# Attention of the first chunk: the masked product of the turned probabilities on VectorE from PSUM instead of on GpSimd

## The reference

```python
dist = BLOCK + qi - si
valid = (dist >= 0) & (dist < WINDOW) & ((blk - 1) * BLOCK + si >= 0)
...
s = s - slopes[:, :, None, None] * dist.astype(jnp.float32)
s = jnp.where(valid, s, NEG_INF)
p = jax.nn.softmax(jnp.concatenate([s, sink_col], axis=-1), axis=-1)[..., :-1]
return jnp.einsum('...kgqs,...skd->...qkgd', p, v.astype(jnp.float32))
```

## Time and profile before

| what | value |
| --- | --- |
| median of 3 runs | 1970.55 us (1965.48 to 1975.21) |
| the profiled execution's own time | 1968.85 us |
| its span, first to last instruction | 1967.1 us |
| PE busy over the span | 1907.0 us (97%) |
| DVE, ACT, POOL busy | 1093.1 (56%), 898.1 (46%), 684.0 us (35%) |
| mean granted TensorE clock | 0.991 |

### The profile page before, as it was taken

The page is one execution under the profiler, slowest core; times in us unless marked ns, Lnnn a source line. Parts: engine busy times, 40 slices in busy tenths (PEclk is TensorE's granted clock), DMA queues, the critical chain, the costliest instruction groups (busy, mean ns, idle before and its releaser), DMA issues.

```text
span 1967.1 us, 27562 instructions
## 1 busy us (share of the span) xinstructions
PE 1907.0 (97%) x10556; PEld 1712.4 (87%) x10556; DVE 1093.1 (56%) x1889; ACT 898.1 (46%) x1794; POOL 684.0 (35%) x605
## 2 busy tenths in 40 slices
PE   7989999999999999999999999999999999999997
PEld 4767887687889998899999879999997999999796
DVE  7974416755693417546833474694337459441834
ACT  6764435645573214445732353573225347431532
POOL 0135675876122123521221262222126222212531
PEclk9999999999999998999999999999999999999998
DMA  6667885377676773466767526776763676777255
GB/s 231 246 236 264 300 311 164 129 279 252 244 263 207 262 253 131 151 236 253 279 229 275 212 108 247 266 271 240 280 222 107 229 282 244 256 274 249 103 207 177
DMA packets 110482, 451.01 MB, mean 229 GB/s; under 512 B 14836, under 2 KB 55060, under 8 KB 66324
## 3 DMA queue, kind: packets, MB, share of 16 engines
q1 hardware_dynamic: 110352, 449.25, 63.8%
HBM read 362.69 MB, written 86.52 MB: 228 GB/s over the span
## 4 chain that ended last, share of the span: by engine, by line
PE 76%; DVE 11%; ACT 4%; DMA 3%; issue 3%; POOL 2%; SPq 0%; POOLq 0%; DVEq 0%; ACTq 0%
PE psum L1337 66%; PE psum L1425 3%; PE psum L1393 3%; PE psum L1408 2%; DVE conv_out L1027 2%; DMA w_stage<-w_big 1%; DMA w_split<-w_cache 1%; PE psum L1369 1%; DVE inv_rms L996 1%; DVE lru_or_o L1060 1%; POOL w_split L597 1%; DVE scores L1126 1%; DVE resid L1096 1%; DVE gate_i L1044 1%; PE psum L1349 1%
## 5 line engine op out<-in xcount | busy, mean ns | idle before, releaser
L1337 PE MATMUL psum<-b_hi,w_split 128*128 128x384 f32 (+2 forms) x2880 | 811.0, 355 | 7.8 <-POOL b_lo L627 3.8
L1337 PE MATMUL psum<-a_hi,w_split 128*128 128x384 f32 (+2 forms) x2560 | 722.1, 356 | 11.7 <-DVE a_lo L990 6.7
L1337 PEld LDWEIGHTS psum<-b_hi,w_split 128*128 128x128 f32 x2880 | 532.9, 189 | 60.9 <-issue 23.1
L1337 PEld LDWEIGHTS psum<-a_hi,w_split 128*128 128x128 f32 x2560 | 472.0, 188 | 45.5 <-issue 12.6
L1337 PE MATMUL psum<-b_lo,w_split 128*128 128x384 f32 (+2 forms) x1440 | 504.7, 350 | 0.0
L1337 PE MATMUL psum<-a_lo,w_split 128*128 128x384 f32 (+2 forms) x1280 | 447.4, 350 | 0.0
L606 POOL TENSOR_TENSOR square_sum<-square_sum,square 128x384 f32<-128x384 f32 (+2 forms) x140 | 155.4, 1110 | 427.1 <-ACT square L769 427.1
L1337 PEld LDWEIGHTS psum<-b_lo,w_split 128*128 128x128 f32 x1440 | 272.3, 189 | 11.8 <-issue 0.4
L1337 PEld LDWEIGHTS psum<-a_lo,w_split 128*128 128x128 f32 x1280 | 241.2, 188 | 17.9 <-issue 4.2
L616 POOL TENSOR_TENSOR gate_tanh<-gate_tanh,lru_or_o 128x384 f32<-128x384 f32 (+1 forms) x80 | 87.1, 1090 | 337.0 <-DVE gate_tanh L1079 330.7
L769 ACT ACTIVATE square<-resid 128x384 f32<-128x384 f32 (+2 forms) x140 | 77.4, 553 | 261.0 <-DVE resid L1252 173.6
(11 more groups left out here) (169 smaller groups left out, 2479.8 us busy)
## 6 DMA issues: line engine op xcount, KB each, us to landing
w_split<-w_cache SPq DMA_DIRECT2D x272, 1024.0 KB, 4.8
w_cache<-w_split SPq DMA_DIRECT2D x68, 1024.0 KB, 6.6
w_stage<-w_big SPq DMA_DIRECT2D x68, 512.0 KB, 5.6
w_split<-w_cache_small SPq DMA_DIRECT2D x64, 256.0 KB, 4.4
x_stage<-x SPq DMA_DIRECT2D x32, 192.0 KB, 5.5
resid<-x SPq DMA_DIRECT2D x4, 1536.0 KB, 9.8
y_out<-resid SPq DMA_DIRECT2D x3, 1536.0 KB, 10.3
w_cache_small<-w_split SPq DMA_DIRECT2D x16, 256.0 KB, 6.2
```

The source lines that it names most:

```text
L1337: ins = nc.tensor.matmul(bank(g, c), W[:, s, w, k, :], x[:, k, 0:tt], start=(k == 0 and n == 0), stop=(k == nk - 1 and n == 2))
```

## The change

In the first chunk `keep_old` leaves POOL's program. DVE's program gets a `keep_old` of its own, which reads the turned probabilities from the PSUM bank that ACT copies from, and not from ACT's copy. It waits for the same semaphore, ACT's copy of the unit, and counts up the same one, `pt_old`. It stands after the scores of u + 2 and ahead of the unit's gate work. The other four chunks are left as they were.

```diff
@@ block.gpsimd, attention(g) @@
-                    keep_old(g, u)
+                    if g:
+                        keep_old(g, u)
@@ block.vector @@
+            def keep_old(g, u):
+
+                dve.wait_ge(pt_ready.sem, pt_ready.at(g, event(g, u) + 1))
+                v.tensor_tensor(PT[:, 1, :].rearrange("p (i q) -> p i q", i=4),
+                                PSUM[:, 6 + u % 2, :].rearrange("p (i q) -> p i q", i=4),
+                                OLD_T[:].unsqueeze(1).to_broadcast([128, 4, BLK]), ALU.mult).then_inc(pt_old.sem, 1)
@@ block.vector, attention(g) @@
                     if u + 2 < nu:
                         unit_scores(g, u + 2)
+                    if g == 0:
+                        keep_old(g, u)
                     if u - 3 in whole:
                         silu(g, KT + whole[u - 3])
```

## The result

The changed kernel takes 1975.98 us (median of 13 runs, 1974.54 to 1979.41) against 1970.43 for the kernel before (13 runs, 1965.48 to 1975.21). The ratio is 1.0032, its 95% interval 1.0024 to 1.0040: within the half per cent that the prediction calls no change, but the interval excludes 1, so the change costs about 5.5 us. The profiled execution has a span of 1972.9 us (before 1967.1) and a mean granted clock of 0.989 (0.991). "Turn u" is the start of unit u's turn on PE.

The account below looks back on a forecast made before the run. PE was taken as the bound (76% of the chain, period 4.79 us). Terms 0.74 + 3.60 + 1.67 + 1.3 - 1.13 - 1.73 = +4.45 us gave 1973.3 to 1975.0, forecast 1974 us (chance 0.50), range 1964 to 1982.

Parts of the forecast that it names:

- divide of unit 1, held (turn 1): First chunk: unit 0's weight split runs first on POOL and DVE's next divide waits for it; next turn +1.67 us.
- units 3 and 8, two gate operations (turns 4, 9): DVE's queue with product and two gate operations: ready at 5.16 us against a period of 4.79; +0.74 us for both.
- units 5 and 10, held divide (turns 6, 11): POOL's split starts when silu ends and holds the next divide, 1.80 us late each; +3.60 us for two.
- unit 13, gate product ahead of the divide: POOL's second gate product starts within 0.05 us of DVE's divide; whichever is first, about +1.3 us.
- late POOL products, units 6 and 14: PE's waits ahead of these units' values for POOL's late product disappear: -1.13 and -1.73 us.
- The product's price: Each 128x512 product on DVE takes 0.69 us, like the residual add, 0.60 in the queue; none above 0.75.
- The overtaking splits: Without the product POOL's weight splits start before DVE's divides in units 0, 5 and 10: +1.67 and +3.60 us.
- Units 2 and 7: No gate work, so DVE's divide is due 0.18 us ahead of POOL's split: no cost, but narrowly.
- all splits win: Rival, chance 0.13: units 2 and 7 also lose their 0.18 us, 1.58 each; +7.6 us, 1976.5 to 1978.2.
- DVE becomes the bound: Rival, chance 0.12: the product costs 1.364 us on DVE, from POOL's exclusion or the broadcast; +12.9 us, 1981.7 to 1983.4.
- Only the gain: Rival, chance 0.25: divides go ahead of splits in units 0, 5, 10 and 13; -1.8 us, 1967.0 to 1968.7.
- I pass the shift on whole: After the stage: the output projection moves along with PE's last unit, so the stage's whole +4.45 us reaches the kernel's time.

Follow-up runs that it names:

- the new order of PE alone: Kernel before, product still on POOL, with PE doing the values of u - 1 ahead of the turn of u in the first chunk: 1971.96 us, ratio 1.0018.

## Why the prediction was right, and what it left out

The time came out 2 us above the forecast, by the forecast's mechanism: the medians differ by 5.55 us, the sum had 4.45. Each term, as the distances between turns show it in the profile after against the profile before, in us:

| term | predicted | measured |
| --- | --- | --- |
| divide of unit 1, held (turn 1) | +1.67 | +1.76 |
| units 3 and 8, two gate operations (turns 4, 9) | +0.74 | +0.74 |
| units 5 and 10, held divide (turns 6, 11) | +3.60 | +3.49 |
| unit 13, gate product ahead of the divide | +1.3 | +1.38 |
| late POOL products, units 6 and 14 | -2.86 | -2.94 |
| a late divide of before, turn 12 | none | -0.22 |
| clock behind turns 6 and 11 | none | +3.12 |
| sum of the rows (the stage itself: +7.35) | +4.45 | +7.33 |

The nearness is partly luck. The sum leaves out the clock's 3.12 us, and in this pair of profiles some of that was given back outside the stage, by a fall of the clock in the kernel before (below). Two readings of the prediction are off without harm: turn 1 of before is at 320.04 in the timeline (320.11 is the chain's piece), by which the divide of unit 1 costs 1.74, nearer to the 1.76 measured; and the 0.691 that it calls one of the product's own rows is the residual add's.

- **The product's price** was right: 0.681 to 0.692 us for all 16, none above 0.75. The estimate by the Trainium skill (VectorE: DVE Perf Modes, The TRN2 errata), 0.065 us more from PSUM, is not seen: an unheld divide from SBUF takes the same 0.69.
- **The overtaking splits** were right in place and size, and the experiments show that they are the cause: with the split or the product moved behind the divide they are gone.
- **Unit 13**, the one open order, went to POOL by 0.04 us and gave the distance of 5.66 that was reckoned for that case.
- **Units 2 and 7** kept their margin of 0.18 us. With the product doubled they lost it, and each then cost what the rival "all splits win" put on it (1.6 us measured, 1.58 reckoned).
- **"DVE becomes the bound"** falls: no product was held, not even inside a split (0.68 us with the product behind the divide).
- **"Only the gain"** falls for this order of instructions, and with it, as a forecast of the kernel's time, the rule that the Trainium skill (GPSIMD Engine Reference, Engine selection) gives for elementwise work. The product is twice as fast on DVE, as the rule has it, and the kernel is slower. With the product behind the divide a gain of 0.14% appears, hardly clear of noise.
- **The missing step** is what PE's stops do to PE afterwards. I costed a late turn at the length of its stop and took the matmuls behind it at full speed. Two of them were followed by 5 us at a clock of 0.65 to 0.70, +3.12 us in one profile and about +1.5 in the other. The trace of the kernel before has two such stops, 1.72 us ahead of unit 0 and 1.73 ahead of the values of unit 14, and the clock stays behind both, so a fall could not be read from it with any certainty, but a rival with this price was due.
- **"I pass the shift on whole"** is borne out only roughly. In the first pair of profiles the first chunk's last sum of squares, which PE makes within chunk 1's projections, moved by 7.3 us (505.51 to 512.81; the stage itself had started 0.68 later), and the span grew by 5.8. In the repeated pair the stage is 5.75 us longer and the span 9.1 (1964.5 and 1973.6), so what lies outside the stage differs by some us from one execution to the next. In the first pair 1.6 us of it can be located, right behind that sum. First the stop and the window of before, then of after, with 20 matmuls each:

```profile
508.63 2.33 issue
510.00:517.00 7.00, 6.05 (x20) 4.81 (x21) 2.21 (x6) 0.41 (x1) 0.00 (x0) 0.76 0.76 259
```

```profile
515.91 2.18 issue
517.50:522.50 5.00, 4.41 (x20) 3.70 (x21) 2.02 (x5) 0.40 (x1) 0.00 (x0) 1.00 0.65 226
```

At this place it was the kernel before that ran at a lower clock (0.76 against 1.00), 6.05 us of PE against 4.41 for the same work: the clock fell behind its stop of 2.33 us and not behind the other's of 2.18.

Still open: what decides whether the clock falls. All 14 profiles have a stop of 1.72 us just ahead of unit 0, where PE's scores wait for DVE; in seven of them the clock falls around the start of unit 0, and not in the two of the kernel before. Of the other 13 stops of 1.66 to 1.73 us in the stage, three were followed by a fall (turns 6 and 11 of the changed kernel, turn 6 of its repeat). The three stops of 2.32 to 2.37 us with the doubled product and those of 3.24 and 3.25 us with the values first on the kernel before were all followed by one; of the two of 2.14 there, one was. Behind the shorter stops of the stage (0.54 to 1.56 us) none was seen that doesn't also stand just behind the 1.72 ahead of unit 0. So a fall can follow a stop of 1.7 us and need not, and each makes a stage's time in one profile uncertain by 1 to 1.5 us. No kernel here changed the clock alone.

## What to carry to other kernels

Work taken off an engine that is not on the chain is still an edit to the chain's timing: what stood behind it in that engine's queue now starts earlier and can take a shared resource ahead of the instruction that the chain waits for. Before moving it, list for each unit which of the two is issued first afterwards, and by how much; where the chain's instruction loses, put the moved work behind it (here that turned +0.3% into -0.1%). And see whether the bound engine can do something else first, and measure the two edits together: in the first chunk the move alone (1.0032) and the new order of PE alone (1.0018) each cost time, and both together gained (0.9983).

## What the hardware showed unexpectedly

- The nine gate matmuls took 2.27 us behind the values (64 output columns) and 2.08 behind the turn (128), 0.19 to 0.20 us in every period, in chunk 1 too. Why is not shown. PE's weight loading stands idle for 0.38 us behind the values in either order, ahead of the gate before and ahead of the turn now; the 0.17 us of idle time between turn and values is what is gone. No run measured a pair of shapes by itself.
- A stop of 1.7 us can be followed by 1.5 us more, through the granted clock; one of 3.24 was followed by values at 0.50 that took 1.98 us instead of 1.02. Stops of 0.6 us at turns 6 and 11 were not followed by a fall.
- A divide held by an instruction of POOL ended 0.55 us behind it in each pair read (unit 5: 348.02 and 348.57; the doubled product's unit 2: 334.44 and 334.99; before).
